# Expert stage of a hybrid decoder layer: rows turned in 32x32 blocks by VectorE, weights laid out by partition

## The reference, cut to what matters

```
p_group = softmax(x @ router_group_w + b);  g_w, g_idx = top_k(p_group, 1)            # 1 of 4 groups
e_w, e_idx = top_k(softmax(logits of that group), 2)                                  # 2 of its 8 experts
slots: every (token, expert) pair gets a place in a block of its expert
yb = (silu(xe @ w1[e]) * (xe @ w3[e])) @ w2[e]                                        # w1, w3: 1024x512, w2: 512x1024
y  = sum over a token's two slots of gate * yb;  out = rms_norm(h + y) * norm_final_g
```

## Time and profile before

| | us |
|---|---|
| median of 3 runs | 3241.54 (3239.69 to 3244.01) |
| the profiled execution's own time | 3252.22 |
| its span | 3250.4 |
| PE busy, share of the span | 2960.2 (91%) |
| DVE busy | 1269.0 (39%) |
| ACT busy | 1036.3 (32%) |
| `up` of W1 and W3 (L2705), four groups | 152.2 + 147.9 + 154.3 + 146.9 |
| W2 products (L2721) | 301.3 |
| turning X (L2698), turning hidden rows (L2712) | 55.2, 35.9 |

### The profile page before, as it was taken

The page is one execution under the profiler, slowest core; times in us unless marked ns, Lnnn a source line. Parts: engine busy times, 40 slices in busy tenths (PEclk is TensorE's granted clock), DMA queues, the critical chain, the costliest instruction groups (busy, mean ns, idle before and its releaser), DMA issues. The chain is left out here.

```text
span 3250.4 us, 71261 instructions
## 1 busy us (share of the span) xinstructions
PE 2960.2 (91%) x29293; PEld 1978.0 (61%) x29294; DVE 1269.0 (39%) x3129; ACT 1036.3 (32%) x2103; POOL 293.1 (9%) x321
## 2 busy tenths in 40 slices
PE   5999999999978988879999699978999999999990
PEld 3676667666747877768787655545555555555540
DVE  3554455445423333327676566661111111111118
ACT  3354235423423444336555533411111111111102
POOL 0000000000000000104332000001000000000004
PEclk8999999999989999999999899989999999999995
DMA  7132212211131222227788565317678676776658
GB/s 254 64 107 86 88 68 97 93 49 56 56 96 39 74 62 66 60 75 239 223 225 186 172 202 157 109 58 283 236 278 278 242 278 225 252 277 225 212 188 321
DMA packets 287252, 516.53 MB, mean 159 GB/s; under 512 B 95026, under 2 KB 109234, under 8 KB 282916
## 3 DMA queue, kind: packets, MB, share of 16 engines
q1 hardware_dynamic: 245708, 390.43, 36.4%
q10 hardware_dynamic: 25128, 66.26, 6.6%
q0 software_dynamic: 16176, 56.37, 4.9%
HBM read 394.99 MB, written 118.01 MB: 158 GB/s over the span
## 5 line engine op out<-in xcount | busy, mean ns | idle before, releaser
L299 PE MATMUL proj_main_ps<-proj_xt,proj_w 128*128 128x257 f32 x1536 | 349.6, 379 | 0.0
L299 PEld LDWEIGHTS proj_main_ps<-proj_xt,proj_w 128*128 128x128 f32 x1536 | 288.6, 190 | 41.0
L2721 PE MATMUL moe_y_ps<-moe_w,moe_ht 128*64 128x512 f32 x1312 | 301.3, 601 | 3.2 <-ACT moe_ht L2760 3.2
L2478 PE MATMUL out_proj_ps<-out_w,out_ct 128*128 128x512 f32 x544 | 241.8, 598 | 6.1 <-DMA out_w<-in_w_out_dram 6.1
L364 PE MATMUL proj_main_ps<-proj_w,proj_xt 128*128 128x512 f32 x512 | 225.3, 593 | 0.0
L2771 ACT ACTIVATE moe_sg<-moe_gate 128x256 f32<-128x256 f32 x82 | 31.5, 384 | 538.2 <-PE moe_gate L2705 538.2
L2721 PEld LDWEIGHTS moe_y_ps<-moe_w,moe_ht 128*64 128x64 f32 x1312 | 87.3, 137 | 158.9 <-issue 155.4
L2807 DVE COPY moe_y<-moe_y_ps 128x512 f32<-128x512 f32 x82 | 56.7, 692 | 314.2 <-PE moe_y_ps L2721 314.2
L2478 PEld LDWEIGHTS out_proj_ps<-out_w,out_ct 128*128 128x128 f32 x544 | 101.6, 192 | 122.0 <-issue 121.2
L364 PEld LDWEIGHTS proj_main_ps<-proj_w,proj_xt 128*128 128x128 f32 x512 | 97.0, 190 | 108.6 <-issue 107.1
L2756 ACT COPY moe_xt<-moe_xt_ps 128x512 f32<-128x512 f32 x83 | 48.6, 586 | 333.4 <-PE moe_xt_ps L2698 333.4
(11 more groups left out here) (408 smaller groups left out, 5047.6 us busy)
## 6 DMA issues: line engine op xcount, KB each, us to landing
moe_w<-in_expert_w_dram SPq DMA_DIRECT2D x64, 2048.0 KB, 8.9
kept_first_gate<-in_expert_w_dram SPq DMA_DIRECT2D x16, 2048.0 KB, 11.0
kept_first_up<-in_expert_w_dram SPq DMA_DIRECT2D x16, 2048.0 KB, 15.8
y_rows<-moe_y ACTq DMA_DIRECT2D x164, 128.0 KB, 5.8
ft_p<-proj_uf SPq DMA_DIRECT2D x32, 642.0 KB, 3.3
y_rows<-ahead_feat POOLq DMA_DIRECT2D x33, 512.0 KB, 6.0
rwkv_feat<-ft_p SPq DMA_DIRECT2D x48, 321.0 KB, 3.0
att_s_k<-in_cache_att_k_dram ACTq DMA_DIRECT2D x14, 1024.0 KB, 8.5
```

Of the source, the lines that this page charges most:

```text
L299: last = mm(out[:, 0:w + 1], W[:, k, kind * C + m * P:kind * C + (m + 1) * P], XT[n % 2][:, k, 0:w + 1], start=(k == 0), stop=(k == KT - 1))
L2478: last = mm(proj_ps[j][:], CT[t % 2][:, k, :], W[:, k, 512 * j:512 * (j + 1)], start=(k == 0), stop=(k == KT - 1))
L2721: last = mm(py[j * HB:(j + 1) * HB, :], HT[:, c, r * HB:(r + 1) * HB], W2[s][:, k, j * 512:(j + 1) * 512], start=(k == 0), stop=(k == FE / ...
```

## The change

Expert rows are no longer turned by TensorE. VectorE has a transpose that turns each 32x32 block by itself, and the layouts on both sides of it are changed so that this is enough.

- The table of `dispatch` lists quarter rows (256 floats): partition 32q+t of column b holds 4*token+q for places 0 to 31, column b+132 the same for places 32 to 63. It is built by eight products for each column of pairs where there were two, each with 32 stationary columns. Its two DVE steps have 264 columns in place of 132.
- POOL copies two index columns and issues two gathers for each block, 128 quarter rows each.
- VectorE's `turn_x` turns X to XT with one instruction of 512 elements in each partition. Its input is read with a step of 8 floats, so that XT's partition p holds elements 8p to 8p+7 of the rows. For this the weights are loaded as `(p k) n`: partition p holds rows 8p to 8p+7 of W1 and W3, and rows 4p to 4p+3 of W2.
- The product with p3 is written by eight instructions of 32 partitions by 128 elements, which deal the hidden rows to the four partition quarters (HQ), and one more transpose of 256 elements makes HT.
- In SBUF each weight row is followed by a gap of 8 floats.
- TensorE loses six transposes for each block, ScalarE the two copies out of PSUM. TensorE waits for `gated` before W1's product and for `dealt` before W3's.
- VectorE's order in a block is: sigmoid times p1, `turn_x` of the next block (after `h3`), the eight products, the copy of the last block's result, the transpose of the hidden rows.

```
+XB = 32
+PAD = 8
...
-    half = np.repeat(np.arange(2), HB)[:, None]
+    quarter = np.repeat(np.arange(P // XB), XB)[:, None]
     row = lambda n: np.broadcast_to(np.arange(n), (P, n))
-    return np.ascontiguousarray(np.concatenate([row(HB), row(NBC), 2 * np.repeat(token, 2, 1), half], 1).astype(np.float32))
+    return np.ascontiguousarray(np.concatenate([row(HB), row(NBC), P // XB * np.repeat(token, 2, 1), quarter], 1).astype(np.float32))
...
-        rows = sb("rows", [P, NBC])
+        rows = sb("rows", [P, 2 * NBC])
...
-            sp.dma_start(W1, w1[0].rearrange("(k p) n -> p k n", p=P)).then_inc(loaded, 16)
-            sp.dma_start(W3, w3[0].rearrange("(k p) n -> p k n", p=P)).then_inc(loaded, 16)
+            sp.dma_start(W1, w1[0].rearrange("(p k) n -> p k n", p=P)).then_inc(loaded, 16)
+            sp.dma_start(W3, w3[0].rearrange("(p k) n -> p k n", p=P)).then_inc(loaded, 16)
...
-                    v.tensor_scalar(HOTP[:, n, :], places, place[:, n:n + 1], token2[:, n:n + 1], ALU.is_equal, ALU.mult).then_inc(at_token, 1)
+                    v.tensor_scalar(HOTP[:, n, :], places, place[:, n:n + 1], token4[:, n:n + 1], ALU.is_equal, ALU.mult).then_inc(at_token, 1)
             v.wait_ge(listed, 1)
-            v.tensor_scalar(rows[:], table[:, 0:NBC], half, None, ALU.add).then_inc(step, 1)
+            v.tensor_scalar(rows[:], table[:, 0:2 * NBC], quarter, None, ALU.add).then_inc(step, 1)
...
-                    for j in range(2):
-                        last = nc.tensor.matmul(table[j * HB:(j + 1) * HB, 0:NBC], HOTP[:, n, :], HOTB[:, n, :], start=(n == 0), stop=(n == NA - 1), skip_group_check=True)
+                    for h in range(2):
+                        for j in range(P // XB):
+                            last = nc.tensor.matmul(table[j * XB:(j + 1) * XB, h * NBC:(h + 1) * NBC], HOTP[:, n, h * XB:(h + 1) * XB], HOTB[:, n, :],
+                                                    start=(n == 0 and h == 0), stop=(n == NA - 1), skip_group_check=True)
...
-        W1 = [first_w1, sb("w1_1", [P, KT, FE])]
-        W3 = [first_w3, sb("w3_1", [P, KT, FE])]
-        W2 = [sb(f"w2_{s}", [P, FE // P, D]) for s in range(2)]
+        W1 = [first_w1, sb("w1_1", [P, KT, FE + PAD])[:, :, 0:FE]]
+        W3 = [first_w3, sb("w3_1", [P, KT, FE + PAD])[:, :, 0:FE]]
+        W2 = [sb(f"w2_{s}", [P, FE // P, D + PAD])[:, :, 0:D] for s in range(2)]
         ident = sb("ident", [P, P])
-        X, XT = sb("x", [P, D // 2]), sb("xt", [P, KT // 2, P])
-        SG, HD, HT, Y = sb("sg", [P, HF]), sb("hd", [P, HF]), sb("ht", [P, 2, P]), sb("y", [P, D // 2])
+        X, XT = sb("x", [P, 2, D * XB // P]), sb("xt", [P, KT, HB])
+        SG, HD, HQ, HT, Y = sb("sg", [P, HF]), sb("hd", [P, HF]), sb("hq", [P, 2, P]), sb("ht", [P, FE // P, HB]), sb("y", [P, D // 2])
...
-                one = lambda w: w[bass.ds(e, 1), :, :].rearrange("o (k p) n -> p (o k) n", p=P)
-                sp.dma_start(W1[s][:], one(w1)).then_inc(w13_ld[s], 16)
-                sp.dma_start(W3[s][:], one(w3)).then_inc(w13_ld[s], 16)
+                one = lambda w: w[bass.ds(e, 1), :, :].rearrange("o (p k) n -> p (o k) n", p=P)
+                sp.dma_start(W1[s], one(w1)).then_inc(w13_ld[s], 16)
+                sp.dma_start(W3[s], one(w3)).then_inc(w13_ld[s], 16)
 
             def down(e, s):
-                sp.dma_start(W2[s][:], w2[bass.ds(e, 1), :, :].rearrange("o (k p) n -> p (o k) n", p=P)).then_inc(w2_ld[s], 16)
+                sp.dma_start(W2[s], w2[bass.ds(e, 1), :, :].rearrange("o (p k) n -> p (o k) n", p=P)).then_inc(w2_ld[s], 16)
...
-            sp.wait_ge(x_ld, 16)
+            sp.wait_ge(x_ld, 32)
...
-            def turn_x(b):
-                pe.wait_ge(x_ld, 16 * b + 16)
-                if not start_of_all(b):
-                    pe.wait_ge(xt_ready, b)
-                for k in range(KT // 2):
-                    last = nc.tensor.transpose(px[:, k * P:(k + 1) * P], X[:, k * P:(k + 1) * P], ident[:])
-                last.then_inc(x_turned, 1)
...
+                        last = mm(bank[j * HB:(j + 1) * HB, 0:HF], XT[:, k, :], W[:, k, j * HF:(j + 1) * HF],
...
-            def turn_hidden_before(b):
-                pe.wait_ge(hidden, b)
-                for c in range(2):
-                    last = nc.tensor.transpose(ph[:, c * P:(c + 1) * P], HD[:, c * P:(c + 1) * P], ident[:])
-                last.then_inc(h_turned, 1)
...
+                        last = mm(py[j * HB:(j + 1) * HB, :], HT[:, k, :], W2[s][:, k, j * 512:(j + 1) * 512],
...
-                    pe.wait_ge(hidden, b)
+                    pe.wait_ge(gated, b)
                 up(p1, W1[s]).then_inc(h1, 1)
                 if not start_of_all(b):
-                    turn_hidden_before(b)
+                    pe.wait_ge(dealt, b)
                 up(p3, W3[s]).then_inc(h3, 1)
-                turn_x(b + 1)
...
-            turn_x(0)
             end = over_experts(pe, step)
-            turn_hidden_before(end)
...
-            def xt(b):
-                a.wait_ge(x_turned, b + 1)
-                if not start_of_all(b):
-                    a.wait_ge(h3, b)
-                nc.scalar.copy(XT[:].rearrange("p k t -> p (k t)"), px[:]).then_inc(xt_ready, 1)
-
-            def ht_before(b):
-                a.wait_ge(h_turned, b)
-                nc.scalar.copy(HT[:].rearrange("p k t -> p (k t)"), ph[:, 0:2 * P]).then_inc(ht_ready, 1)
...
-                    ht_before(b)
-                xt(b + 1)
...
-            half_rows = hn.rearrange("n (a d) -> (n a) d", a=2)
+            quarter_rows = hn.rearrange("n (a d) -> (n a) d", a=P // XB)
 
             def load_x(b):
-                nc.gpsimd.tensor_copy(IX[:], IDX[:, bass.ds(b, 1)]).then_inc(ix_ready, 1)
+                nc.gpsimd.tensor_copy(IX[:, 0:1], IDX[:, bass.ds(b, 1)])
+                nc.gpsimd.tensor_copy(IX[:, 1:2], IDX[:, bass.ds(b + NBC, 1)]).then_inc(ix_ready, 1)
                 g.wait_ge(ix_ready, b + 1)
                 g.sem_inc(go, 1)
-                g.indirect_dma_start(X[:], None, half_rows, bass.IndirectOffsetOnAxis(ap=IX[:], axis=0)).then_inc(x_ld, 16)
+                for h in range(2):
+                    g.indirect_dma_start(X[:, h, :], None, quarter_rows, bass.IndirectOffsetOnAxis(ap=IX[:, h:h + 1], axis=0)).then_inc(x_ld, 16)
 
             def step(b, s, i, first):
-                g.wait_ge(x_turned, b + 2)
+                g.wait_ge(xt_ready, b + 2)
                 load_x(b + 2)
 
             load_x(0)
-            g.wait_ge(x_turned, 1)
+            g.wait_ge(xt_ready, 1)
...
+            def turn_x(b):
+                v.wait_ge(x_ld, 32 * b + 32)
+                if not start_of_all(b):
+                    v.wait_ge(h3, b)
+                v.transpose(XT[:].rearrange("p k (h t) -> p h k t", h=2), X[:].rearrange("p h (i k) -> p h k i", k=KT)).then_inc(xt_ready, 1)
+
             def step(b, s, i, first):
                 v.wait_ge(sig, b + 1)
-                if not start_of_all(b):
-                    v.wait_ge(h_turned, b)
                 v.tensor_tensor(HD[:], SG[:], p1[:, 0:HF], ALU.mult).then_inc(gated, 1)
                 v.wait_ge(gated, b + 1)
+                turn_x(b + 1)
                 v.wait_ge(h3, b + 1)
-                v.tensor_tensor(HD[:], HD[:], p3[:, 0:HF], ALU.mult).then_inc(hidden, 1)
+                for j in range(2):
+                    for a in range(2):
+                        for h in range(2):
+                            rows, cols = slice(j * HB + h * XB, j * HB + (h + 1) * XB), slice(a * P, (a + 1) * P)
+                            last = v.tensor_tensor(HQ[(2 * j + a) * XB:(2 * j + a + 1) * XB, h, :], HD[rows, cols], p3[rows, cols], ALU.mult)
+                last.then_inc(dealt, 1)
                 if not start_of_all(b):
                     evacuate_before(b)
+                v.wait_ge(dealt, b + 1)
+                v.transpose(HT[:].rearrange("p k (h t) -> p h k t", h=2), HQ[:].rearrange("p h (i k) -> p h k i", k=FE // P)).then_inc(ht_ready, 1)
+            turn_x(0)
...
```

More of the change, by code:

```diff
@@ L2562, in dispatch @@
         places, numbers = cn[:, 0:HB], cn[:, HB:HB + NBC]
-        token2, half = cn[:, HB + NBC:HB + NBC + NA], cn[:, HB + NBC + NA:]
+        token4, quarter = cn[:, HB + NBC:HB + NBC + NA], cn[:, HB + NBC + NA:]
         bi = sb("block_int", [P, NA], I32)
@@ L2629, in experts @@
         w2_ld = [sem(f"down_loaded{s}") for s in range(2)]
-        x_ld, x_turned, xt_ready = sem("x_loaded"), sem("x_turned"), sem("xt_ready")
-        h1, h3, sig, gated, hidden = sem("h1_done"), sem("h3_done"), sem("sigmoid_done"), sem("gated_done"), sem("hidden_ready")
-        h_turned, ht_ready, y_done = sem("h_turned"), sem("ht_ready"), sem("y_done")
+        x_ld, xt_ready = sem("x_loaded"), sem("xt_ready")
+        h1, h3, sig, gated, dealt = sem("h1_done"), sem("h3_done"), sem("sigmoid_done"), sem("gated_done"), sem("hidden_dealt")
+        ht_ready, y_done = sem("ht_ready"), sem("y_done")
         y_ev, y_st = sem("y_copied"), sem("y_stored")
```

(20 more changed lines are left out.)

5 lines of the change are left out of this document (1 added, 4 removed).

## The result

| | before | after |
|---|---|---|
| median, us | 3240.61 (4 runs, 3234.14 to 3244.01) | 3140.78 (4 runs, 3130.04 to 3142.11) |
| span of the profiled execution | 3250.4 | 3139.1 |
| PE busy | 2960.2 | 2859.9 |
| DVE busy | 1269.0 | 1551.4 |
| ACT busy | 1036.3 | 962.0 |

The ratio is 0.9686, with a 95% interval of 0.9666 to 0.9706: about 100 us faster, where 3148 had been predicted. The two profiled executions are 111 us apart, 11 more than the medians. That part is not the change's: the stage before `dispatch`, whose code is the same, already ended 11.4 us earlier (the first issue of W1 at 2171.71 against 2183.09). So I compare distances between landmarks of one execution.

A forecast was written before the change was run, and what follows sets the result against it. TensorE's start-to-start block time, times 82 blocks, was taken to bound the expert stage. 3252.22 - 98.4 + 7 + 1 - 3 = 3158.8 us for the profiled execution; the median, 10.7 below, was predicted at 3148, range 3128 to 3180.

The forecast's parts named there:

- A block on TensorE: Expert stage: a block without transposes is 1.20 us shorter (bounds 0.96 and 1.32), 98.4 us off over 82 blocks.
- rival 5: Expert stage: the shape change was free, only 0.96 us a block goes, 3168 us; 10 in 100.
- VectorE keeps up: Expert stage: VectorE's work is 5.0 of 10.4 us a block, `turn_x` 1.06 under 2.4 us of cover; costs nothing.
- Rival 1: Expert stage: VectorE becomes the bound, `turn_x` takes 4.2 us and XT comes 0.9 us late, 3222 us; 4 in 100.
- The gathers: Expert stage: second gather issued about T + 3.5 (T: W3's product ends), landing 3.8 to 7.9 us; hidden, 1.4 us spare.
- Rival 2: Expert stage: gathers come late, landing of 12 us in 32 blocks, 86 us on, 3234 us; 4 in 100.
- Weight loads, order and gap at zero: Expert stage: weight loads have 5.5 us to spare; their new memory order and the gap cost zero.
- rival 3: Expert stage: loads become the bound, at a rate of 200 GB/s 270 us on, 3511 us; 3 in 100.
- Dispatch: Table products in `dispatch`: 544 records, 31 ns each after the half-clock start, 7 us on (2 to 22).
- Rival 4: `dispatch`: records do not overlap four-wide, 63 ns each, 15 us more than forecast, 3163 us; 6 in 100.
- Table to first product: From the table's end to the first W1 product: transposes and ScalarE's copy go, other steps come, 1 us on (0 to 2).
- The end: Last W2 product: waits 1.3 us for VectorE's copy and transpose where it started 3.17 late; 3 us off (0 to 4).

The follow-up runs named there:

- each half: Against the kernel before: only X turned by VectorE, 3187.52 us, ratio 0.9856; only the hidden rows turned by VectorE, 3195.96 us, ratio 0.9873.

## Why the prediction was right, point by point

- **A block on TensorE**: 1.20 us off predicted, 1.26 found; 82 x 1.26 = 103.3 against 98.4 (C to Y holds 81 distances and the tail, and shrank by 103.83). I had taken every boundary as costly as W2's to W1's, 3.48 us. The three are 3.43 to 3.46, so a little more of the change of shape was in that row too. The bounds of 0.96 and 1.32 held, and rival 5 (only the transposes' own time) falls: each half saved 0.15 more than it owned.
- **VectorE keeps up**: `turn_x` takes 1.11 us (1.06 taken), the eight products 2.32 (2.3 at most), the turn to HT 0.65 (0.53). HT was needed late and PE waited for it only at the end, 1.54 us. Rival 1 falls. But its sentence, that 3.4 us for `turn_x` would cost nothing, was wrong: one transpose more, 2.1 us in all ahead of XT, cost 39. It counted TensorE's cover and left out that the gather of the next X starts only when `turn_x` ends.
- **The gathers**: the second is issued 3.64 us after `turn_x` starts (3.5 predicted) and lands within 8.0 us (7.9 taken as worst); hidden, as forecast. I took that worst for rare; in the changed kernel landings of 6.3 to 8.0 us were the rule in the blocks where `turn_x` waited, against a median of 3.8 over all blocks before. `turn_x` waited for it in 39 blocks of the stretch shown. Rival 2 was nearer than its 4 in 100 says.
- **Weight loads, order and gap at zero**: right for the change as it is: with neither the time was the same, 3138.76. The gap alone is not worth zero. Without it, the same order costs 37 us, and the forecast of 3148 would have missed by 30. The gap was part of the change and I gave no reason for it, so that this term held was luck. The runs of 16 KB "for a partition" stood in my text, but I looked only at the rate (rival 3, which falls: no PE wait for a load, 321 GB/s in the window), not at what else waits in the queues.
- **Dispatch**: +7 predicted, +7.96 found. The second run has 315 records in 9.19 us, 29 ns each, where I took 31. Against that, TensorE idled 1.50 us between its two runs, which I had not counted. Rival 4 falls. The Trainium skill (TensorE: Matmul & The Clock Gate, the section on 56 against 53.3 ns) gives its 62 ns for a matmul with hardware decode off. From it I had estimated 34 us for the 544 records, and the table's products took 19.4 with the idle time. Whether the rule counts records or products (two records, 58 ns here) the table does not tell; the 22 ns a record of the earlier trace rows, 43 a product, lie under it either way.
- **Table to first product**: +0.2 for +1.
- **The end**: -1.7 between Y and E, where the last product takes 3.65 for 5.35, and -1.6 before Y, since that product waited 1.54 us for 3.17: -3.3 for -3. Against it stands a term that I had left out, +1.5. The first block of the stage has no W2 product and became 0.8 us shorter, not 1.26, and a later one came 0.9 late. (The 6.1 us that I gave for the first W1 product were 6.32 from start to start before, and are 5.54 now.)
- **The profiled execution** was to be put 10.7 us above the median, and the forecast from it, 3148, lies 7 above the result. 5 of these are the block's term; the others nearly cancel (within 1 us), and the rest is the scatter of the medians.

## What to carry to other kernels

When work moves to another engine, check two lengths: the cover on the bound engine, and the ring through the buffer that the moved step frees (its own time, the index copy, the issues, the landing) against the period. The shorter slack decides, and here it was the ring's. A layout that makes runs in memory longer can make transfers of another queue late; the count of packets by size on the profile's page shows it before a wait does.

## What the runs showed of the hardware

- Rows of a destination with a gap of 32 bytes went as packets of 2 and 4 KB, touching rows that also touch in memory as one of 16 KB. At the same bytes, and where VectorE waited for them, half of the gathers beside them (32 of 61) landed 8.2 to 9.2 us after issue, where none had taken more than 8.0.
- `turn_x`'s 512 elements a partition, read with a step of 8 floats, took 1.11 us; the 256 of HT, with a step of 4, took 0.65. The Trainium skill (Vector Engine (DVE) Microarchitecture Reference, section 3.8) has one element per cycle per lane, from which I had estimated 0.53 for the first: twice that was measured. Whether the step or the type costs it, no run here separates.
- Eight VectorE instructions on 32 partitions each took 278 ns for 128 elements, one after the other, although they touch different quarters.
- A change between products of 64-column tiles and transposes of 128 columns cost 0.15 us beyond the transposes' own time, in either place (a block of 10.86 and 11.08 us with one run of transposes each, 10.34 with none).
- With the 16 idle products TensorE lost the 2.4 GHz level again after 1.93 us of idling in the second block (granted clock 0.50 in the window from 2200 us), and had it back in the window from 2204 us. The length of such an idle time did not decide it alone: without the gap, 2.17 us before the W1 product at 2241.60 cost the level (5.36 us, clock 0.50), while 2.58 us before the one at 2813.01 did not (3.67 us, clock 1.00).
